# The scan's stage: output casts, a tap of the convolution, the crossing tile's copy and the gate on ScalarE, VectorE's row in another order

## What is computed

```python
def token_mixer(...):
    ...                      # q, f, k, v per head; chunked scans forward and backward give o_f, o_b
    g, sb, sc, sh, ga, gb = jnp.split(z_rest, ...)      # products of h with w_in
    o = o_f + o_b
    o = o * lax.rsqrt(jnp.mean(o * o, axis=-1, keepdims=True) + EPS) * a_norm_g
    y_a = o.reshape(bn, L, A_WIDTH) * jax.nn.silu(g)
    y_b = sb * short_conv_1d(sc * sh, sconv_w)          # w0*up[:-2] + w1*up[1:-1] + w2*up[2:]
    merged = jax.nn.sigmoid(ga) * (y_a @ w_pa) + jax.nn.sigmoid(gb) * (y_b @ w_pb)
    return merged @ w_o, s_f, s_b
```

## Time and profile before

| | us |
|---|---|
| median of 3 runs (2338.88 to 2342.0) | 2340.42 |
| the profiled execution's own time | 2341.36 |
| its span | 2339.6 |
| TensorE busy in the span | 2269.1 |
| VectorE busy | 1648.1 |
| ScalarE busy | 985.2 |

### The profile page before, as it was taken

The page is one execution under the profiler, slowest core; times in us unless marked ns, Lnnn a source line. Parts: engine busy times, 40 slices in busy tenths (PEclk is TensorE's granted clock), DMA queues, the critical chain, the costliest instruction groups (busy, mean ns, idle before and its releaser), DMA issues.

```text
span 2339.6 us, 48669 instructions
## 1 busy us (share of the span) xinstructions
PE 2269.1 (97%) x18378; PEld 2182.1 (93%) x18378; DVE 1648.1 (70%) x2555; ACT 985.2 (42%) x1370; POOL 8.4 (0%) x18
## 2 busy tenths in 40 slices
PE   4899999999999999989999999999999999999999
PEld 3678888999999999989999999999999999999999
DVE  3465565899986666888887888875556766676764
ACT  3322222455444343445444444444445444444442
POOL 0000000000000000000000000000000000000000
PEclk7999999999999999999999999999999999999999
DMA  9956455433446667994555554555556444444443
GB/s 383 419 210 236 187 205 214 173 126 143 143 177 254 238 251 267 338 362 162 182 186 188 188 189 179 179 195 188 188 184 213 156 164 147 154 150 159 146 176 130
DMA packets 69511, 475.62 MB, mean 203 GB/s; under 512 B 7728, under 2 KB 9776, under 8 KB 18384
## 3 DMA queue, kind: packets, MB, share of 16 engines
q1 hardware_dynamic: 68688, 467.59, 54.6%
q0 software_dynamic: 768, 7.26, 0.8%
HBM read 469.58 MB, written 5.24 MB: 203 GB/s over the span
## 4 chain that ended last, share of the span: by engine, by line
PE 82%; DVE 9%; issue 2%; ACT 1%; DVEq 1%; ACTq 0%
PE acc L764 78%; PE aux L764 3%; DVE lo L1125 3%; DVE ar L1342 1%; DVE qla L1335 1%; DVE sc L1314 1%; DVE tt L1340 0%; DVE qlb L1335 0%; DVE raw L1135 0%; PE aux L1020 0%; DVE yab L1141 0%; ACT hi L460 0%; DVE yab L1142 0%; DVE hxu L1142 0%; ACT n L635 0%
## 5 line engine op out<-in xcount | busy, mean ns | idle before, releaser
L1125 DVE TENSOR_TENSOR lo<-raw,hi 128x1024 fp32r<-128x1024 f32 (+1 forms) x716 | 812.3, 1168 | 194.7 <-ACT hi L460 190.9
L460 ACT ACTIVATE hi<-raw 128x1024 fp32r<-128x1024 f32 (+1 forms) x716 | 695.7, 1012 | 313.8 <-PE acc L764 256.4
L764 PE MATMUL acc<-hx,hi 128*128 128x256 f32 (+1 forms) x3072 | 661.0, 312 | 4.3 <-DVE lo L1125 3.8
L764 PEld LDWEIGHTS acc<-hx,hi 128*128 128x128 f32 x3072 | 495.0, 188 | 40.8 <-issue 6.9
L764 PE MATMUL acc<-hxu,hi 128*128 128x256 f32 x2816 | 502.7, 282 | 7.5 <-DVE hxu L1142 7.4
L764 PE MATMUL acc<-hx,lo 128*128 128x256 f32 (+1 forms) x1536 | 473.4, 308 | 0.0
L764 PEld LDWEIGHTS acc<-hxu,hi 128*128 128x128 f32 x2816 | 432.4, 189 | 8.8 <-issue 7.5
L764 PE MATMUL acc<-hxu,lo 128*128 128x256 f32 x1408 | 394.6, 280 | 0.0
L764 PE MATMUL acc<-u,hi 128*128 128x272 f32 (+1 forms) x2048 | 382.3, 287 | 0.0
L764 PEld LDWEIGHTS acc<-u,hi 128*128 128x128 f32 x2048 | 317.3, 188 | 4.5 <-issue 2.5
L764 PEld LDWEIGHTS acc<-hx,lo 128*128 128x128 f32 x1536 | 288.8, 188 | 17.5
(11 more groups left out here) (293 smaller groups left out, 2292.9 us busy)
## 6 DMA issues: line engine op xcount, KB each, us to landing
raw<-wts SPq DMA_DIRECT2D x390, 1024.0 KB, 4.9
raw<-wdown SPq DMA_DIRECT2D x64, 704.0 KB, 4.1
xc<-xct SPq DMA_DIRECT2D x1, 4096.0 KB, 12.6
rawx<-wts SPq DMA_DIRECT2D x2, 1024.0 KB, 28.9
x<-xct SPq DMA_DIRECT2D x1, 2048.0 KB, 10.0
park<-x POOLq DMA_DIRECT2D x1, 2048.0 KB, 10.8
xf<-park POOLq DMA_DIRECT2D x1, 2048.0 KB, 9.3
outt<-outs SPq DMA_DIRECT2D x16, 128.0 KB, 3.7
```

The lines of the kernel that those rows point to most:

```text
L460: A.activation(HI[:, slot, a:b, 0:P], RAW[:, p % 4, a:b, :], ACT.Copy).then_inc(hi_half, 1)
L764: return pe.matmul(*a, **k)
L1125: V.tensor_tensor(LO[:, slot, a:b, 0:P], RAW[:, p % 4, a:b, :], HI[:, slot, a:b, 0:P].bitcast(F32), ALU.subtract).then_inc(lo_half, 1)
```

## The change

- On ScalarE: `mix_border` (the rounding of y_b and the crossing tile's copy, both of the head before) stands behind the six refilling copies; high split 3 stands ahead of the gate; the gate is one silu from PSUM into GS, and frees the bank; the rounding of y_a (`mix_ya_high`) stands behind it; the middle tap of the convolution (a copy scaled by w1) stands behind high split 4. The table sets are silu and log/exp instead of sigmoid and log/exp, and the first silu load stands ahead of head 0.
- On VectorE: the two roundings, the middle tap, the crossing copy and the gate's product are gone. The difference of y_b of the head before opens the head, then KS, and only then low split 1. YT stands ahead of masked copy 2 with no wait on its result, its difference behind low split 3. UP stands behind level 4, the two remaining taps behind low split 4 and behind level 6.
- New semaphores: tap_ready, yb_high, ya_made, ya_high. gate_sig no longer counts the heads.

The diff, with the unchanged lines cut:

```diff
...
-CHAIN = {"v_rec": 7, "v_mix": 21, "v_merge": 4, "v_up": 16, "v_attn": 22, "a_mix": 3, "a_attn": 4}
+CHAIN = {"v_rec": 7, "v_mix": 17, "v_merge": 4, "v_up": 16, "v_attn": 22, "a_mix": 3, "a_attn": 4}
...
         yb_ready, mrg_ready = sem("yb_ready"), sem("mrg_ready")
+        tap_ready, yb_high, ya_made, ya_high = (sem(n) for n in ("tap_ready", "yb_high", "ya_made", "ya_high"))
         in_x1, x1_chunk, sq2_done, ss2_mm, rs2_done, n2_ready, h2_aff, hx2_ready, x1_out, zero_set = (
...
+            def mix_border(i):
+                x = lambda d: YAB[:, d, bass.ds(i, 1), 0:T].rearrange("p a t -> p (a t)")
+                act.wait_ge(bank_free, prod_index("mix", i, 3) + 1)
+                A.activation(x(2), SCB[:], ACT.Copy).then_inc(yb_high, 1)
+                act.wait_ge(tile_mm, 9 * i + LEVELS + 1)
+                act.wait_ge(tile_read, 9 * i + LEVELS)
+                A.activation(SC[:].rearrange("p s (t n) -> p (s t) n", t=2)[:, 1:3, :],
+                             AUX[:, 1, 0:T].rearrange("p (t n) -> p t n", t=2), ACT.Copy).then_inc(tile_read, 1)
+            def mix_ya_high(i):
+                x = lambda d: YAB[:, d, bass.ds(i, 1), 0:T].rearrange("p a t -> p (a t)")
+                act.wait_ge(ya_made, i + 1)
+                A.activation(x(0), YT[:], ACT.Copy).then_inc(ya_high, 1)
             def mix_head(i, peeled):
...
                 A.activation(TT0[:, 2, :], f[:, 0, :], ACT.Copy).then_inc(hd_init, 1)
+                if not peeled:
+                    mix_border(i - 1)
                 hi("mix", i, 2)
...
                     mix_norm(i - 1)
-                    tables(SIGMOID)
+                    tables(SILU)
+                hi("mix", i, 3)
                 done("mix", i, 0)
                 act.wait_ge(bank_free, prod_index("mix", i, 0))
-                A.activation(SGG[:], ACC[:, 0, 0:T], ACT.Sigmoid).then_inc(gate_sig, 1)
-                tables(LOGEXP)
-                hi("mix", i, 3)
+                if not peeled:
+                    act.wait_ge(ya_made, i)
+                A.activation(GS[:], ACC[:, 0, 0:T], ACT.Silu).then_inc(bank_free, 1)
+                if not peeled:
+                    mix_ya_high(i - 1)
                 done("mix", i, 1)
...
                 A.activation(SCB[:], ACC[:, 1, 0:T], ACT.Copy).then_inc(bank_free, 1)
+                tables(LOGEXP)
                 hi("mix", i, 4)
-
+                act.wait_ge(bank_free, prod_index("mix", i, 2) + 1)
+                A.activation(SGG[:], UP[:, 1:T + 1], ACT.Copy, scale=vcd("sconv", HEADS + i)).then_inc(tap_ready, 1)
+            tables(SILU)
             mix_head(0, True)
...
                     if peeled and jj == 0:
+                        mix_border(HEADS - 1)
                         mix_norm(HEADS - 1)
...
                     A.activation(GB[:], ACC[:, (b + 1) % 4, 0:T], ACT.Sigmoid).then_inc(gate_sig, 1)
+                    if peeled and jj == 0:
+                        mix_ya_high(HEADS - 1)
                     hi("merge", i, p + 4)
...
-            GSIG = GSIG + HEADS + 2 * KD
+            GSIG = GSIG + 2 * KD
...
                 dve.wait_ge(on_tr, i + 1)
-                link(V.scalar_tensor_tensor(YT[:], AUX[:, 2, T:2 * T], vc("anorm"), GS[:], ALU.mult, ALU.mult))
-                split_small(x(0), x(1), YT[:]).then_inc(ya_ready, 1)
+                V.scalar_tensor_tensor(YT[:], AUX[:, 2, T:2 * T], vc("anorm"), GS[:], ALU.mult, ALU.mult).then_inc(ya_made, 1)
+            def mix_ya_low(i):
+                x = lambda d: YAB[:, d, bass.ds(i, 1), 0:T].rearrange("p a t -> p (a t)")
+                dve.wait_ge(ya_high, i + 1)
+                V.tensor_tensor(x(1), YT[:], x(0).bitcast(F32), ALU.subtract).then_inc(ya_ready, 1)
+            def mix_yb_low(i):
+                x = lambda d: YAB[:, d, bass.ds(i, 1), 0:T].rearrange("p a t -> p (a t)")
+                dve.wait_ge(yb_high, i + 1)
+                V.tensor_tensor(x(3), SCB[:], x(2).bitcast(F32), ALU.subtract).then_inc(yb_ready, 1)
...
                 dve.wait_ge(tile_mm, need)
-                if n == LEVELS:
-                    V.tensor_copy(SC4[:, 1:3, :], AUX[:, 1, 0:T].rearrange("p (t n) -> p t n", t=2)).then_inc(tile_read, 1)
-                    return
                 dve.wait_ge(o_mm if n == 0 else tile_read, free)
...
-                x = lambda d: YAB[:, d, bass.ds(i, 1), 0:T].rearrange("p a t -> p (a t)")
                 qf = QF[:, bass.ds(i, 1), :].rearrange("p a t -> p (a t)")
...
                 if not peeled:
-                    tile_copy(i - 1, 8)
-                lo("mix", i, 1)
+                    mix_yb_low(i - 1)
                 dve.wait_ge(hd_init, i + 1)
...
                 V.tensor_tensor(KS[:], QK[:, 1, :], QK[:, 3, :], ALU.add).then_inc(ks_ready, 1)
+                lo("mix", i, 1)
                 level(0)
...
                 level(3)
+                if not peeled:
+                    mix_ya(i - 1)
                 tile_copy(i, 2)
...
                 if not peeled:
-                    mix_ya(i - 1)
-                    dve.wait_ge(ya_ready, 1 + i)
-                dve.wait_ge(gate_sig, GSIG + i + 1)
-                V.tensor_tensor(GS[:], ACC[:, 0, 0:T], SGG[:], ALU.mult).then_inc(bank_free, 1)
+                    mix_ya_low(i - 1)
                 tile_copy(i, 3)
                 level(4)
+                done("mix", i, 2)
+                dve.wait_ge(bank_free, prod_index("mix", i, 2))
+                V.tensor_tensor(UP[:, 1:T + 1], ACC[:, 2, 0:T], SCB[:], ALU.mult).then_inc(bank_free, 1)
                 tile_copy(i, 4)
...
                 lo("mix", i, 4)
+                dve.wait_ge(tap_ready, i + 1)
+                link(V.scalar_tensor_tensor(SGG[:], UP[:, 0:T], w(0), SGG[:], ALU.mult, ALU.add))
                 tile_copy(i, 5)
                 level(6)
+                link(V.scalar_tensor_tensor(SGG[:], UP[:, 2:T + 2], w(2), SGG[:], ALU.mult, ALU.add))
                 tile_copy(i, 6)
...
                 V.tensor_tensor(QS[:], AR[:, 0:3:2, :], qf.unsqueeze(1).broadcast_to([P, 2, T]), ALU.mult).then_inc(qs_ready, 1)
-                done("mix", i, 2)
-                dve.wait_ge(bank_free, prod_index("mix", i, 2))
-                V.tensor_tensor(UP[:, 1:T + 1], ACC[:, 2, 0:T], SCB[:], ALU.mult).then_inc(bank_free, 1)
-                dve.wait_ge(bank_free, prod_index("mix", i, 2) + 1)
-                link(V.tensor_scalar(SGG[:], UP[:, 1:T + 1], w(1), None, ALU.mult))
-                link(V.scalar_tensor_tensor(SGG[:], UP[:, 0:T], w(0), SGG[:], ALU.mult, ALU.add))
-                link(V.scalar_tensor_tensor(SGG[:], UP[:, 2:T + 2], w(2), SGG[:], ALU.mult, ALU.add))
                 done("mix", i, 3)
...
                 dve.wait_ge(bank_free, prod_index("mix", i, 3) + 1)
-                split_small(x(2), x(3), SCB[:]).then_inc(yb_ready, 1)
                 tile_copy(i, 7)
...
             ch.leave(ITERS["mix"] - 1, "v_mix")
-            GSIG += HEADS
...
                     if first:
-                        tile_copy(HEADS - 1, 8)
+                        mix_yb_low(HEADS - 1)
                     lo("merge", i, p + 1)
...
                         mix_ya(HEADS - 1)
+                        mix_ya_low(HEADS - 1)
                         dve.wait_ge(ya_ready, 1 + HEADS)
...
```

## The result

The changed kernel takes 2345.57 us (median of 11 runs, 2342.7 to 2346.28), the one before 2341.66 (11 runs in the same comparison): ratio 1.0016, 95% interval 1.0009 to 1.0024. It is 3.9 us or 0.16% slower. That is inside the 0.2% that I called no change, and yet clear of noise and outside my range, which ended at 2344.8. The profiled execution took 2346.28.

The account below looks back on a forecast made before the run. VectorE's row was taken as the bound. Head 0 +4.61, six heads -3.30, last head -1.21, merge stage +0.1 gave +0.2: 2341.6 us profiled, 2340.7 as median. Range 2336.5 to 2344.8; no change 0.80.

Parts of the forecast that it names:

- Z to A: VectorE from QS's start (Z) to the first instruction after the last masked copy (A): 4.76 us falling to 3.84.
- table load ahead of head 0: ScalarE's extra silu table load before head 0 delays hd_init: +1.28 us.
- KS to QS of head 0: VectorE in head 0: split 1 behind KS +2.26, gate product -0.33, UP and two taps +0.34, +0.62, +0.62.
- QS to A, head 0: VectorE from head 0's QS to the first instruction after its last masked copy: 4.02 to 3.84, -0.18 us.
- A of head 1 to A of head 7: Six steady heads, between first instructions after the last masked copy: 6 x -0.55 = -3.30 us.
- A of head 7 to the outputs: Last head: VectorE bounds up to level 4's product, only the saving of 1.21 us counts; TensorE runs alone after.
- Z + 3.84: Loop: y_b's difference starts 3.84 us behind QS, after ScalarE's six copies, y_b's cast (0.40) and hand-over (0.05).
- A to Z: VectorE from the first instruction after the last masked copy to the next QS: 26.24 us growing to 26.61.
- step "head 0": Head 0: table load and split 1 behind KS, +4.79 us at QS; head 1's first instruction 4.61 us later.
- UP waits for product 2: Rival, chance 0.09: moved UP waits for product 2 in eight heads; margin 0.2 us at most; 2347 at 0.8 a head.
- the wait is not there: Rival, chance 0.08: ScalarE's cast is ready when VectorE comes, TensorE bounds the head at 29.53 us; 2332.7.
- third rival: Rival, chance 0.03: unlinked VectorE instructions are no cheaper than waiting ones, +3.2 us, 2343.9.

Follow-up runs that it names:

- e2_head0_only: The changed kernel with VectorE's split of product 1 ahead of KS in head 0 alone: 2341.80 us.
- e3_fill: The changed kernel with eleven additional float32 matmuls on TensorE between head 0's same-tile matmuls and level 0, result unused: 2344.79 us.
- e1_split_first: The changed kernel with VectorE's split of product 1 ahead of y_b's difference and KS in all heads: 2329.66 us.
- e5_crossing_early: The changed kernel with split 1 first, the first silu load behind head 0's copies, and the crossing copy behind the second refilling copy: 2326.79 us.
- e6_ks_ahead: The changed kernel with KS first, then the split of product 1, then y_b's difference: 2342.02 us.
- e8_before_ks_ahead: The kernel before with one reordering, KS ahead of the split of product 1: 2343.46 us.

## Why the prediction was wrong

The mechanism in the loop was right: VectorE idles ahead of y_b's difference for 2.4 us a head (2.1 predicted), the head moves little though 1.7 us of VectorE's busy time leave it, and the last stretch is as worked out. But the heads win only 0.22 us each, and head 0 loses far more than they win. Two steps failed: the size of Z to A in the loop, and head 0, in which TensorE's rate was taken for given. By the steps of the prediction, from the profile's starts:

| step | predicted | measured | how |
|---|---|---|---|
| table load ahead of head 0 | +1.28 | +1.50 | KS - copy of ST: 437.23 - 430.94, against 434.91 - 430.12 |
| KS to QS of head 0 | +3.51 | +4.83 | 464.11 - 437.23, against 456.96 - 434.91 |
| QS to A, head 0 | -0.18 | +0.05 | 468.18 - 464.11, against 460.98 - 456.96 |
| A of head 1 to A of head 7 | -3.30 | -1.32 | 652.86 - 468.18 = 184.68, against 6 x 31.00 |
| A of head 7 to the outputs | -1.21 | -1.18 | 683.27 - 652.86, against 678.57 - 646.98 (460.98 + 6 x 31.00) |
| sum | +0.1 | +3.88 | |

The other 0.1 us of the predicted +0.2 belongs to the merge stage, behind these outputs. Of the 3.8 us between the sums, 2.0 come from the six heads, 1.3 from KS to QS of head 0, 0.2 from the table load and 0.2 from QS to A.

- **The term Z + 3.84** was mis-sized by 0.23 us, and it counts in every head. I had the hand-over from ScalarE's cast to VectorE at 0.05 us; in the loop it takes 0.27 (the cast at 498.29 + 0.40, the difference at 498.96). The two taps with a wait on their own result took 0.69 and not 0.62 (490.12 to 490.81 on VectorE), and A to Z became 26.71 for 26.61. Both together give 30.78 for 30.45, 2.0 us over six heads. My bounds for the cast, 0.1 each way, took in neither.
- **The step "head 0"** failed in what it left out. I worked out that VectorE would lose 3.5 us there from KS to QS, and without the wait at UP it lost 3.3 (the two taps cost 0.51 each in this straight code, and not 0.62). But I followed TensorE only as far as its matmuls would start later, and took their rate for given. The standstill of 2.28 us brought the clock down, product 1's first half took 4.45 us (441.16 to 445.61) where it takes 2.89 in e2_head0_only (438.73 to 441.62), and so product 2 reached UP 1.56 us late, at a place where I had put the margin at 0.2 us. The clock's part of the 1.56 is 1.2: with the clock at 1.00, in e3_fill and e2_head0_only, 0.36 of the wait is left, so the margin was mis-sized in head 0 too. The prediction had named a wait above 0.5 at UP as a sign of being wrong. Its rival "UP waits for product 2" had the right place, but expected the wait in all heads and did not have the clock as its cause; in the steady heads there is no such wait after the change. e2_head0_only and e3_fill show the cause.
- **The pitches held.** y_a's product has a pitch of 0.39 without a wait behind it (480.94 to 481.33), where 0.40 was taken, UP one of 0.33 (485.90 to 486.23), where 0.34 was: the Trainium skill's rule on the drain ("VectorE: DVE Perf Modes", section "The DRAIN you can't avoid") is again not what this trace shows, and the rival built on it falls. The same section of the Trainium skill adds that a next instruction "that is not held starts earlier", which the prediction left out and which these rows fit. The table load took 1.28 us and delayed the head by 1.4 to 1.5. The Trainium skill, "ScalarE: Activation LUTs", section "What ACT_TABLE_LOAD costs", has a drain of another 1.38; it is not there in this trace.
- The rival "the wait is not there" fell as a forecast, and e1_split_first shows its worth: with the wait covered the kernel is at 2329.66, where I had priced it at 2332.7 with head 0's loss still in it. TensorE's busy time of 29.53 us, which the prediction took for the least that a head can take, was no such floor: the head takes 29.01 us there, and 28.84 in e5_crossing_early.
- Two slips changed no term of the sum. The chances add up to 1.02, and the third rival's 2343.9 stands among the cases slower by over 0.2%, though it is only 3.2 us above the forecast. And VectorE's head has a second gap with a releaser, 0.16 us ahead of y_b's rounding, where the prediction read only one.

The range was too narrow by the two terms together. It held 0.1 to 0.3 us a head each way, which the 0.33 a head used up, and about 1 us for head 0, which lost 1.8 more than predicted, with nothing set aside for the clock.

## What to carry to other kernels

When work leaves the engine that sets the pace, ask what that work covered: KS depended on ScalarE's six copies before the change too, and VectorE's own steps hid it. Where an instruction waits for another engine's chain, put independent work ahead of it and price the hand-over from a row of the loop and not of straight code; here one split of 2.27 us in front of two waits was worth 15.9 us. Where a reordering makes TensorE stand still, read the granted clock of the next few microseconds, for the matmuls behind it may run at half rate, as they did here for 3.4 us.

## What the runs showed that was not expected

- A standstill of 2.28 us behind another short one of 0.41 (437.29 to 437.70) was enough for the granted clock to fall to 0.50. It fell about 1.1 us after TensorE had started again (0.91 in 441 to 442, the start at 440.69). In e6_ks_ahead the same two standstills, of 0.39 and 2.28 us, brought it down half a microsecond before TensorE started again (0.82 in 440.00 to 440.25, the start at 440.68), and it was low for 3.4 us there too. In e8_before_ks_ahead, with one standstill of 1.50 us, it did not fall. What decides between these cases was not tried.
- A wait in a loop costs VectorE more than in straight code. A dependent tap and what follows it are 0.51 us apart in head 0 (459.81 to 460.32), 0.69 in the loop (490.12 to 490.81), and the difference of y_b starts 0.27 us behind the cast's end in the loop, where the one of the last head, which stands outside it, starts 0.11 behind (cast at 680.62 + 0.42, difference at 681.15) and had VectorE's own row ahead of it. KS of head 0, which does wait, starts 0.11 behind the sixth copy (436.72 + 0.40, 437.23). The waits in the loop are against values that are worked out at run time; that this is the cause is argued, not shown.
